# Six pieces of the second down projection as block products of seven factors, with all sums of quarters on GpSimd

## Chip, cores, metric

One core of a Trainium2 chip runs the whole program. The metric is the device time of one launch in microseconds.

## What is computed

Two transformer blocks, one behind the other, on 256 tokens of width 1024. The change is in the last product of the second one:

```python
def second_block(x, ...):
    ...
        h = h + y @ w_out[l]
        u = _rms(h, ln_ffn_g[l])
        h = h + jnp.square(jax.nn.relu(u @ w_ff1[l])) @ w_ff2[l]
    return h
```

`w_ff1` is 1024 x 4096 and `w_ff2` 4096 x 1024. With `relu(..)**2` called the hidden values (256 tokens x 4096), the last step is a product 256 x 4096 x 1024, added to `h`. All inputs are fp32.

## The kernel before

TensorE multiplies in fp32r. To keep the precision, each operand of the large products is split in two parts, high (the value rounded by a ScalarE copy) and low (the rest, by a VectorE subtraction), and `product3` (from L701; its matmul is L707) issues three matmuls for each product: high x high, high x low, low x high.

**The second down projection** is the stage "down2". Its contraction length 4096 is 32 tiles of 128. Two tiles are a *piece*; there are 16 pieces, called 0 to 15 here (`c` in the code). A piece of weights is 128 partitions x 2048: two k-tiles of 1024 output columns. The weights arrive by SyncE's DMA in chunks of two pieces (2 MB) into three ring slots; a slot is loaded again once both its pieces are split (`pieces_split`).

**ScalarE** (`split_high`, to L1743) writes the high part of a piece into one of two buffers (W_HIGH) when TensorE has read the piece two before (`down2_pieces_read`). **VectorE** (`split_low`, L2318 to L2325) then writes the low part (W_LOW), `weights - W_HIGH`, both operands in SBUF. **TensorE** (`down`, L1082 to L1105) goes over pieces 0 to 13 in order. For each, two k-tiles, four PSUM banks (two token tiles x two halves of 512 output columns), three matmuls of 128x512: 24 matmuls a piece. The last two pieces (14 and 15) are done bank by bank, so that a bank's result can be scaled, added to X and stored while the next is computed.

**Before it** the stage "ffn2" computes the hidden values: `u @ w_ff1` in 32 jobs. Two jobs make two hidden tiles, called q = 0 to 15 here; q belongs to piece q of down2. ScalarE copies half a job's bank, VectorE adds (`add_cross`, L2647) and squares into one of two buffers HF2 (L3179), ScalarE and VectorE split into HID2_HIGH and HID2_LOW (L2254, L2675). In between they split the weights of the next piece, as in down2. GpSimd does nothing in either stage.

Each engine's order is that in which the code is written; semaphores link the engines.

Of the kernel before, what the change touches and what calls it, by code (L numbers as in the profile page):

```python
# [16 lines left out]
F32 = mybir.dt.float32  # L17
# [6 lines left out]
P = 128  # L24
S = 256
# [193 lines left out]
def build(nc, x, weights, params, params2, consts, tables, rel_bias, norm_final, positions, table_dram, out):  # L219
    with ExitStack() as ctx:  # L220
# [240 lines left out]
        def piece_source(k):  # L461

            kind, i, j = PIECES[k]
            width = CHUNKS[CHUNK_AT[kind, i]][2]
            rows = {"branch": 4, "down1": width // D, "down2": width // D}.get(kind, KD)
            w = rings[weight_slots(kind, i)[0]][:, 0:width].rearrange("p (k n) -> p k n", k=rows)
            if kind in ("down1", "down2"):
                return w[:, 2 * j:2 * j + 2, :]
            if (kind, i) in TOKEN_CHUNKS:
                return w[:, 4 * j:4 * j + 4, :]  # L470
            if PIECES[k] in FIRST_HIDDEN:
                return w[:, :, :].rearrange("p k (t j n) -> p k j t n", t=2, j=2)[:, :, j, :, :]
# [137 lines left out]
        def _(pe):  # L610
# [468 lines left out]
                branch_product(i)  # L1079


            def down(kind, high, low, nk, ready, fills):  # L1082
# [12 lines left out]

                for c in range(nk // 2 - 2):
                    for k in range(2):
                        ready(2 * c + k)
                        for b in range(4):
                            ins = part(c, k, b)  # L1100
                    ins.then_inc(sem(kind + "_pieces_read"), 1)
                ready(nk - 1)
                for b in range(4):
                    for c in (nk // 2 - 2, nk // 2 - 1):
                        for k in range(2):  # L1105
                            ins = part(c, k, b)
                    close_fill(ins)
# [552 lines left out]
        def _(act):  # L1660
# [60 lines left out]
            def split_high(k):  # L1721

                if k >= len(PIECES):
                    return
                kind, i, _ = PIECES[k]
                slot, turn = weight_slots(kind, i)
                if PIECES[k] == ("in1", 1, 0):
                    act.wait_ge(sem("second_weights_in"), 16)
                else:
                    act.wait_ge(sem(f"weights_in{slot}"), 16 * turn)  # L1730
                if PIECES[k] == ("in2", 0, 0):
                    act.wait_ge(sem("hidden_split"), FF1_CHUNKS)
# [10 lines left out]
                act.activation(like_source(piece_parts(k)[0], k), piece_source(k), ACT.Copy).then_inc(sem("pieces_high"), 1)  # L1743

            def norm_gains(n, banks=range(4)):

# [519 lines left out]
            hidden2_high(q)  # L2266
            for k in range(PIECE_AT["down2", 0, 0] + 2, len(PIECES)):
                split_high(k)


        @block.vector
        def _(dve):
# [45 lines left out]
            def split_low(k):  # L2318

                if k >= len(PIECES):  # L2320
                    return
                dve.wait_ge(sem("pieces_high"), k + 1)
                high, low = [like_source(part, k) for part in piece_parts(k)]
                dve.tensor_tensor(low, piece_source(k), high.bitcast(F32), ALU.subtract)\  # L2324
                    .then_inc(sem("pieces_split"), 1)  # L2325

            def norm_gains(n, banks=range(4)):

# [875 lines left out]
        def _(pool):  # L3204
# [230 lines left out]
```

## Time and profile before

| | |
|---|---|
| time, median of 3 runs | 931.65 us (931.39 to 932.35) |
| the profiled execution | 931.5 us, its span in the trace 929.6 us |
| granted TensorE clock, mean | 0.999 |
| TensorE busy | 915.3 us (98%) |
| VectorE busy | 626.2 us (67%) |
| ScalarE busy | 486.8 us (52%) |
| GpSimd busy | 65.3 us (7%) |

The span is what the instructions cover; 1.9 us lie around it. A matmul's busy time (0.39 us for 512 columns) overlaps the next one's: the distance of starts tells what one costs. Times in a timeline are microseconds from the span's start.

### The profile page before, as it was taken

The page shows a single profiled execution, that of the slowest core. Times are in us where ns is not written, and L with a number is a line of the kernel's source. Part 1 is how long each engine was busy: PE and PEld are TensorE (multiplying, and loading weights), DVE is VectorE, ACT ScalarE, POOL GpSimd, SP SyncE. Part 2 cuts the span into 40 slices and gives each one's busy share as a digit, 9 for nine tenths or more (in the row PEclk, how much of TensorE's full clock was granted, in tenths as well). Part 3 has the DMA queues.
Part 4 walks back from the last instruction along what each step waited for, and adds up shares of the span by engine and source line. Part 5 has one row for each costly group of instructions (what it writes and reads, how often), then busy time and mean ns, then how long its engine had stood idle before and what let it go on. Part 6 is the DMA issues. An engine that isn't in the chain of part 4 may idle for free.

```text
span 929.6 us, 15708 instructions
## 1 busy us (share of the span) xinstructions
PE 915.3 (98%) x6417; PEld 785.4 (84%) x6417; DVE 626.2 (67%) x1025; ACT 486.8 (52%) x767; POOL 65.3 (7%) x79
## 2 busy tenths in 40 slices
PE   9999999999999999999999999999999999999998
PEld 8999987787778788888888889988987788888886
DVE  5776446566787768777744769579767677775343
ACT  5654345547854465555534665546427455553331
POOL 1000000131004100000000000003450000000000
PEclk9999999999999999999999999999999999999999
DMA  9769852244456435544443432231002345555421
GB/s 326 298 132 278 315 182 91 99 173 146 172 215 235 181 135 204 203 183 183 181 181 129 191 141 91 91 138 47 3 3 74 126 176 195 197 200 210 183 91 45
DMA packets 16870, 149.78 MB, mean 161 GB/s; under 512 B 1744, under 2 KB 6224, under 8 KB 8352
## 3 DMA queue, kind: packets, MB, share of 16 engines
q1 hardware_dynamic: 14688, 140.24, 40.7%
q0 software_dynamic: 1296, 5.24, 3.1%
q10 hardware_dynamic: 816, 3.31, 0.9%
q8 instruction: 51, 0.84, 0.4%
q14 instruction: 19, 0.16, 0.1%
HBM read 144.59 MB, written 4.19 MB: 160 GB/s over the span
## 4 chain that ended last, share of the span: by engine, by line
PE 89%; DVE 4%; ACT 3%; issue 2%; POOL 1%; DVEq 0%; ACTq 0%; POOLq 0%
PE bank L707 46%; PE bank L749 15%; PE bank L751 7%; PE bank L664 4%; PE bank L1509 3%; PE bank L914 1%; POOL HN L3251 1%; PE bank L951 1%; PE bank L988 1%; PE bank L811 1%; DVE W_LOW L2324 1%; PE bank L825 1%; ACT W_HIGH L1743 1%; PE bank L1376 1%; PE bank L1270 0%
## 5 line engine op out<-in xcount | busy, mean ns | idle before, releaser
L2324 DVE TENSOR_TENSOR W_LOW<-weights,W_HIGH 128x2048 fp32r<-128x2048 f32 (+1 forms) x98 | 224.5, 2292 | 141.5 <-ACT W_HIGH L1743 140.8
L1743 ACT ACTIVATE W_HIGH<-weights 128x2048 fp32r<-128x2048 f32 (+1 forms) x98 | 186.4, 1903 | 154.7 <-PE bank L707 153.2
L749 PE MATMUL bank<-OVER_BOTH,W_HIGH 128*128 128x512 f32 x608 | 211.6, 393 | 0.2 <-DVE W_LOW L2324 0.2
L751 PE MATMUL bank<-OVER_BOTH,W_LOW 128*128 128x256 f32 x608 | 170.2, 280 | 0.0
L749 PEld LDWEIGHTS bank<-OVER_BOTH,W_HIGH 128*128 128x128 f32 x608 | 114.2, 188 | 25.8 <-DVE W_LOW L2324 0.5
L751 PEld LDWEIGHTS bank<-OVER_BOTH,W_LOW 128*128 128x128 f32 x608 | 114.2, 188 | 0.0
L707 PE MATMUL bank<-W_HIGH,HID_HIGH 128*128 128x512 f32 x200 | 77.9, 390 | 0.0
L707 PE MATMUL bank<-W_LOW,HID_HIGH 128*128 128x512 f32 x200 | 77.9, 390 | 0.0
L707 PE MATMUL bank<-W_HIGH,HID_LOW 128*128 128x512 f32 x200 | 77.9, 390 | 0.0
L1681 ACT ACTIVATE ARENA<-bank 128x256 f32<-128x256 f32 x76 | 29.0, 383 | 87.2 <-PE bank L751 86.4
L707 PE MATMUL bank<-FIRST_HIGH,W_HIGH 128*128 128x256 f32 x216 | 61.6, 285 | 0.0
L707 PE MATMUL bank<-FIRST_HIGH,W_LOW 128*128 128x256 f32 x216 | 61.2, 283 | 0.0
L707 PE MATMUL bank<-FIRST_LOW,W_HIGH 128*128 128x256 f32 x216 | 61.2, 283 | 0.0
L664 PE MATMUL bank<-HT,weights 128*128 128x256 f32 x240 | 55.4, 383 | 0.0
L707 PE MATMUL bank<-GATE_HIGH,FIRST_HIGH 128*128 128x512 f32 x128 | 52.2, 408 | 1.0 <-DVE RING_LOW L2471 1.0
L707 PE MATMUL bank<-GATE_HIGH,FIRST_LOW 128*128 128x512 f32 x128 | 50.2, 392 | 0.0
L707 PE MATMUL bank<-RING_LOW,FIRST_HIGH 128*128 128x512 f32 x128 | 50.1, 391 | 0.0
L664 PEld LDWEIGHTS bank<-HT,weights 128*128 128x128 f32 x240 | 44.6, 190 | 6.5 <-issue 0.7
L2647 DVE TENSOR_TENSOR ARENA<-bank,ARENA 128x256 f32<-128x256 f32 x76 | 31.9, 421 | 25.1 <-ACT ARENA L1681 25.1
L2471 DVE TENSOR_TENSOR RING_LOW<-weights,GATE_HIGH 128x1024 fp32r<-128x1024 f32 x32 | 39.5, 1234 | 11.2 <-ACT GATE_HIGH L1778 11.2
L707 PEld LDWEIGHTS bank<-W_HIGH,HID_LOW 128*128 128x128 f32 x200 | 37.6, 188 | 7.9
L707 PEld LDWEIGHTS bank<-W_HIGH,HID_HIGH 128*128 128x128 f32 x200 | 37.6, 188 | 7.8
(524 smaller groups left out, 1827.9 us busy)
## 6 DMA issues: line engine op xcount, KB each, us to landing
weights<-weights_dram SPq DMA_DIRECT2D x62, 2048.0 KB, 7.8
weights<-weights_dram SPq DMA_DIRECT2D x3, 1024.0 KB, 9.3
bias_rows_dram<-ARENA POOLq DMA_DIRECT2D x1, 3072.0 KB, 39.3
BIAS<-params_dram ACTq DMA_DIRECT2D x1, 1997.0 KB, 13.6
weights<-weights_dram SPq DMA_DIRECT2D x1, 1664.0 KB, 6.8
weights<-weights_dram SPq DMA_DIRECT2D x1, 1584.0 KB, 7.9
weights<-weights_dram SPq DMA_DIRECT2D x3, 512.0 KB, 5.7
X<-x_dram ACTq DMA_DIRECT2D x2, 512.0 KB, 4.1
```

The source lines that it names most:

```text
L664: ins = pe.matmul(o, w[:, k, a:a + n], HT[:, k, :], start=(k == 0), stop=(k == KD - 1))
L707: ins = pe.matmul(o, left[a][k], right[b][k], start=(first and k == 0 and a + b == 0), stop=(last and k == n - 1 and a == 1))
L749: pe.matmul(o[:, :].rearrange("p (q n) -> p q n", q=2), high, OVER_BOTH[:, :, k, :], start=(k == 0), stop=False, skip_group_check=True)
L751: ins = pe.matmul(o[:, 0:S], low, OVER_HT[:, k, :], start=False, stop=(k == KD - 1), skip_group_check=True)
L811: pe.matmul(BK[0][:, 0:P], zeros, zeros, start=True, stop=True)
L825: ins = pe.matmul(o[:, t * S:(t + 1) * S], w[b][:, k, t * P:(t + 1) * P], first[a][:, k, :], start=(k + a + b + t == 0), stop=(b == 1 and ...
L1509: ins = pe.matmul(o[b:b + HD, n * HD:(n + 1) * HD], left[b:b + HD, 4 * g + n, :], right[b:b + HD, 4 * g + n, :], start=True, stop=True)
L1681: act.activation(CROSS[kind][:, n % 2, :], o[:, 0:S], ACT.Copy).then_inc(sem("cross_by_act"), 1)
L1743: act.activation(like_source(piece_parts(k)[0], k), piece_source(k), ACT.Copy).then_inc(sem("pieces_high"), 1)
L2324: dve.tensor_tensor(low, piece_source(k), high.bitcast(F32), ALU.subtract)\
L2471: dve.tensor_tensor(low, src, high.bitcast(F32), ALU.subtract).then_inc(sem("gate_split"), 1)
L2647: job_out(dve.tensor_tensor(dst[:, half], o[:, S:2 * S], CROSS[kind][:, n % 2, :], ALU.add), (kind, *tile))
```

## The change

A piece is a product of 2 x 2 blocks: the hidden values in quarters a[t][k] (token tile t, k-tile k, 128x128) and the weights in quarters b[k][f] (k-tile k, column half f, 128x512). Before it takes 8 block products. For the pieces 2, 4, 6, 8, 10 and 12 (`SEVEN`) it now takes 7 (Winograd's form), some of them of sums of quarters:

- **GpSimd** computes four sums of hidden quarters (128x128 each) for each of the six, in ffn2, once q's hidden values are ready; and, in down2, four sums of weight quarters (128x512 each), straight from the ring. The third sum reads the first two's results and the fourth the third's, by way of semaphores. It writes them raw into W_RAW; there are two places for weight sums, in HT/HN (place 0) and in the ARENA (place 1). `W_SUMS_AT` gives the six pieces the places 0, 0, 1, 0, 1, 0.
- **ScalarE** splits the hidden sums (one 128x512 copy) and the weight sums (two of 128x1024) as it does all operands, and **VectorE** subtracts as often. A place is written again when the piece that used it was read (`wait_sums_place`). The fourth weight quarter is needed in no product by itself, so the piece's own split shrinks from 2048 to 1536 columns.
- **TensorE** issues 21 matmuls in place of 24 for each of the six: three of the products go straight to down2's banks 4 and 5 and (the last) 6, others are summed over the six pieces in banks 0 to 3. The first three products need no weight sum.
- **At the end** ScalarE copies bank 0 and VectorE adds banks 0 to 3 into X by eight instructions (two sums, six multiply-adds), ahead of the ones that add banks 4 to 7.
- VectorE, before it writes an HF2 buffer again, waits for GpSimd's sums from it too.

```diff
+SEVEN = (2, 4, 6, 8, 10, 12)
...
+        W_SUMS_AT = [0, 0, 1, 0, 1, 0]
...
+        def wait_sums_place(eng, n):
+
+            if n == 0:
+                eng.wait_ge(sem("jobs_written"), len(JOBS))
+            elif n == W_SUMS_AT.index(1):
+                eng.wait_ge(sem("down2_pieces_read"), 4)
+            else:
+                last = max(m for m in range(n) if W_SUMS_AT[m] == W_SUMS_AT[n])
+                eng.wait_ge(sem("down2_pieces_read"), SEVEN[last] + 1)
...
+            def seven_products(c, high, low):
...
+                product(BK[0], hidden(0, 0), weights_at(0, 0), True)
+                product(BK[4], hidden(0, 1), weights_at(1, 0), False)
+                pe.wait_ge(sem("hidden_sums_split"), n + 1)
+                product(BK[5], [part[:, 3, :] for part in hid], weights_at(1, 1), False)
+                for at, o, left in ((0, BK[1], 0), (1, BK[3], 2), (2, BK[2], 1), (3, BK[6], None)):
+                    pe.wait_ge(sem("weight_sums_split"), 2 * n + at // 2 + 1)
+                    ins = product(o, hidden(1, 1) if left is None else [part[:, left, :] for part in hid],
+                                  [part[:, at, :] for part in sums], left is not None)
+                return ins
...
                 for c in range(nk // 2 - 2):
-                    for k in range(2):
-                        ready(2 * c + k)
-                        for b in range(4):
-                            ins = part(c, k, b)
+                    if kind == "down2" and c in SEVEN:
+                        ready(2 * c + 1)
+                        ins = seven_products(c, high, low)
+                    else:
+                        for k in range(2):
+                            ready(2 * c + k)
+                            for b in range(4):
+                                ins = part(c, k, b)
                     ins.then_inc(sem(kind + "_pieces_read"), 1)
...
+                n = seven(k)
+                if n is not None:
+                    high = W_SUMS[W_SUMS_AT[n]][0]
+                    wait_sums_place(act, n)
+                    for q in range(2):
+                        act.wait_ge(sem("weight_sums"), 3 * n + 2 * q + 1)
+                        act.activation(flat(high[:, 2 * q:2 * q + 2, :]), flat(W_RAW[W_SUMS_AT[n]][:, 2 * q:2 * q + 2, :]), ACT.Copy)\
+                            .then_inc(sem("weight_sums_high"), 1)
...
+                if n is not None:
+                    (high, low), sums = W_SUMS[W_SUMS_AT[n]], W_RAW[W_SUMS_AT[n]]
+                    dve.wait_ge(sem("weight_sums"), 3 * n + 3)
+                    for q in range(2):
+                        dve.wait_ge(sem("weight_sums_high"), 2 * n + q + 1)
+                        half = slice(2 * q, 2 * q + 2)
+                        dve.tensor_tensor(flat(low[:, half, :]), flat(sums[:, half, :]), flat(high[:, half, :]).bitcast(F32),
+                                          ALU.subtract).then_inc(sem("weight_sums_split"), 1)
...
+            for n, c in enumerate(SEVEN):
...
+                pool.wait_ge(sem(f"weights_in{slot}"), 16 * turn)
+                wait_sums_place(pool, n)
+                pool.tensor_tensor(sums[:, 1, :], b[1][1], b[0][1], ALU.subtract)
+                pool.tensor_tensor(sums[:, 0, :], b[0][1], b[0][0], ALU.subtract).then_inc(sem("weight_sums"), 1)
+                pool.wait_ge(sem("weight_sums"), 3 * n + 1)
+                pool.tensor_tensor(sums[:, 2, :], b[1][1], sums[:, 0, :], ALU.subtract).then_inc(sem("weight_sums"), 1)
+                pool.wait_ge(sem("weight_sums"), 3 * n + 2)
+                pool.tensor_tensor(sums[:, 3, :], b[1][0], sums[:, 2, :], ALU.subtract).then_inc(sem("weight_sums"), 1)
```

VectorE before, in down2, pieces 3 to 7 (W_LOW_71 and W_LOW_72 are the two buffers of low parts):

```order
L2324 TENSOR_TENSOR W_LOW_71<-weights,W_HIGH_65 128x2048 [waits pieces_high]
L2324 TENSOR_TENSOR W_LOW_72<-weights,W_HIGH_66 128x2048 [waits pieces_high]
L2324 TENSOR_TENSOR W_LOW_71<-weights,W_HIGH_65 128x2048 [waits pieces_high]
L2324 TENSOR_TENSOR W_LOW_72<-weights,W_HIGH_66 128x2048 [waits pieces_high]
L2324 TENSOR_TENSOR W_LOW_71<-weights,W_HIGH_65 128x2048 [waits pieces_high]
```

VectorE of the change at the same place, pieces 3 to 7 (L2411 is `split_low`'s old line, W_SUMS_LOW_120 place 0 and W_SUMS_LOW_122 place 1 of the weight sums):

```order
L2411 TENSOR_TENSOR W_LOW_71<-weights,W_HIGH_65 128x2048 [waits pieces_high]
L2411 TENSOR_TENSOR W_LOW_72<-weights,W_HIGH_66 128x1536 [waits pieces_high]
L2419 TENSOR_TENSOR W_SUMS_LOW_120<-HN,W_SUMS_HIGH_119 128x1024 [waits weight_sums_high,weight_sums]
L2419 TENSOR_TENSOR W_SUMS_LOW_120<-HN,W_SUMS_HIGH_119 128x1024 [waits weight_sums_high]
L2411 TENSOR_TENSOR W_LOW_71<-weights,W_HIGH_65 128x2048 [waits pieces_high]
L2411 TENSOR_TENSOR W_LOW_72<-weights,W_HIGH_66 128x1536 [waits pieces_high]
L2419 TENSOR_TENSOR W_SUMS_LOW_122<-ARENA,W_SUMS_HIGH_121 128x1024 [waits weight_sums_high,weight_sums]
L2419 TENSOR_TENSOR W_SUMS_LOW_122<-ARENA,W_SUMS_HIGH_121 128x1024 [waits weight_sums_high]
L2411 TENSOR_TENSOR W_LOW_71<-weights,W_HIGH_65 128x2048 [waits pieces_high]
```

Behind the low part of each even piece now stand two subtractions of sums, the first of which waits for all of that piece's weight sums, and the next odd piece's low part stands behind them.

GpSimd of the change, the weight sums of pieces 4 and 6 (before, GpSimd has no instruction here):

```order
L3455 TENSOR_TENSOR HN<-weights 128x512 [waits down2_pieces_read,weights_in1]
L3456 TENSOR_TENSOR HN<-weights 128x512
L3458 TENSOR_TENSOR HN<-weights,HN 128x512 [waits weight_sums]
L3460 TENSOR_TENSOR HN<-weights,HN 128x512 [waits weight_sums]
L3455 TENSOR_TENSOR ARENA<-weights 128x512 [waits down2_pieces_read,weights_in2]
L3456 TENSOR_TENSOR ARENA<-weights 128x512
L3458 TENSOR_TENSOR ARENA<-weights,ARENA 128x512 [waits weight_sums]
L3460 TENSOR_TENSOR ARENA<-weights,ARENA 128x512 [waits weight_sums]
```

Piece 4's set (in HN, place 0) waits until piece 2 is read, piece 6's (ARENA, place 1) until piece 3 is read; it stands right behind piece 4's.

ScalarE of the change, pieces 3 to 5 of down2 (before: three copies of 128x2048):

```order
L1811 ACTIVATE W_HIGH_65<-weights 128x2048 [waits down2_pieces_read,weights_in0]
L1811 ACTIVATE W_HIGH_66<-weights 128x1536 [waits down2_pieces_read,weights_in1]
L1819 ACTIVATE W_SUMS_HIGH_119<-HN 128x1024 [waits weight_sums,down2_pieces_read]
L1819 ACTIVATE W_SUMS_HIGH_119<-HN 128x1024 [waits weight_sums]
L1811 ACTIVATE W_HIGH_65<-weights 128x2048 [waits down2_pieces_read,weights_in1]
```

The copy of piece 5 now stands behind two copies that wait for GpSimd.

## Rows read from the trace of the kernel before

**Rows 1.** The page: span, busy time by engine, weight loads (us to landing)

```profile
span 929.6 us, 15708 instructions
...
PE 915.3 (98%) x6417; PEld 785.4 (84%) x6417; DVE 626.2 (67%) x1025; ACT 486.8 (52%) x767; POOL 65.3 (7%) x79
...
weights<-weights_dram SPq DMA_DIRECT2D x62, 2048.0 KB, 7.8
```

**Rows 2.** Chain that ended last, from 740 us: start, us, what

```profile
838.10 87.34 PE bank L707 x384
...
925.46 0.48 DVE X L3195
```

**Rows 3.** Timeline of TensorE in down2: start, us, instruction [idle before it]

```profile
837.93 0.39 PE L707 MATMUL bank<-W_HIGH,HID_HIGH 128*128 128x512 f32 x1
...
843.15 0.39 PE L707 MATMUL bank<-W_HIGH,HID_LOW 128*128 128x512 f32 x1
843.37 0.39 PE L707 MATMUL bank<-W_HIGH,HID_HIGH 128*128 128x512 f32 x1
...
915.45 0.46 PE L707 MATMUL bank<-DOWN_HIGH,HID_HIGH 128*128 128x512 f32 x1
```

**Rows 4.** Timelines of ScalarE and VectorE, end of ffn2 and down2

```profile
843.63 1.92 ACT L1743 ACTIVATE W_HIGH<-weights 128x2048 fp32r<-128x2048 f32 x1 [2.80 <-PE bank L707]
849.07 1.92 ACT L1743 ACTIVATE W_HIGH<-weights 128x2048 fp32r<-128x2048 f32 x1 [3.52 <-PE bank L707]
...
834.80 2.29 DVE L2324 TENSOR_TENSOR W_LOW<-weights,W_HIGH 128x2048 fp32r<-128x2048 f32 x1 [0.65 <-ACT W_HIGH L1743]
...
839.01 0.69 DVE L3179 SCALAR_TENSOR_TENSOR ARENA<-ARENA 128x512 f32<-128x512 f32 x1
...
845.58 2.29 DVE L2324 TENSOR_TENSOR W_LOW<-weights,W_HIGH 128x2048 fp32r<-128x2048 f32 x1 [2.33 <-ACT W_HIGH L1743]
...
913.07 2.28 DVE L2324 TENSOR_TENSOR DOWN_LOW<-weights,DOWN_HIGH 128x2048 fp32r<-128x2048 f32 x1
...
922.69 0.75 DVE L2651 SCALAR_TENSOR_TENSOR X<-bank,STAT,X 128x512 f32<-128x512 f32 x1 [2.04 <-PE bank L707]
925.46 0.88 DVE L3195 SCALAR_TENSOR_TENSOR X<-bank,STAT,X 128x256 f32<-128x256 f32 x2 [2.02 <-PE bank L707]
```

**Rows 5.** Timelines: GpSimd without VectorE beside it; ScalarE on 1024 columns

```profile
200.15 1.97 POOL L3237 TENSOR_TENSOR ARENA<-ARENA 128x384 f32<-128x384 f32 x2 [4.06 <-PE bank L959]
285.97 1.29 POOL L3251 TENSOR_TENSOR HN<-HN,ARENA 128x512 f32<-128x512 f32 x1 [58.31 <-DVE ARENA L2608]
306.39 2.56 POOL L3251 TENSOR_TENSOR HN<-HN,ARENA 128x512 f32<-128x512 f32 x2 [2.83 <-DVE ARENA L2608]
...
292.04 1.04 ACT L1943 ACTIVATE YT_HIGH<-ARENA 128x1024 fp32r<-128x1024 f32 x1
```

**Rows 6.** Timelines of GpSimd and VectorE where both work

```profile
295.47 2.22 POOL L3251 TENSOR_TENSOR HN<-HN,ARENA 128x512 f32<-128x512 f32 x1 [2.82 <-DVE ARENA L2608]
297.65 3.42 POOL L3251 TENSOR_TENSOR HN<-HN,ARENA 128x512 f32<-128x512 f32 x1
178.91 2.98 POOL L3237 TENSOR_TENSOR ARENA<-ARENA 128x384 f32<-128x384 f32 x2 [79.96 <-PE bank L988]
...
286.74 2.68 DVE L2324 TENSOR_TENSOR W_LOW<-weights,W_HIGH 128x2048 fp32r<-128x2048 f32 x1 [0.85 <-ACT W_HIGH L1743]
295.32 1.21 DVE L2590 TENSOR_TENSOR YT_LOW<-ARENA,YT_HIGH 128x1024 fp32r<-128x1024 f32 x1
297.62 2.29 DVE L2324 TENSOR_TENSOR W_LOW<-weights,W_HIGH 128x2048 fp32r<-128x2048 f32 x1 [0.49 <-ACT W_HIGH L1743]
301.17 0.69 DVE L2608 SCALAR_TENSOR_TENSOR ARENA<-ARENA,bank 128x512 f32<-128x512 f32 x1 [0.66 <-POOL HN L3251]
179.73 1.28 DVE L2471 TENSOR_TENSOR RING_LOW<-weights,GATE_HIGH 128x1024 fp32r<-128x1024 f32 x1
```

**Rows 7.** Groups of GpSimd: busy us, mean ns of one, idle before

```profile
L3251 POOL TENSOR_TENSOR HN<-HN,ARENA 128x512 f32<-128x512 f32 x9 | 14.5, 1634 | 66.8 <-DVE ARENA L2608 66.8
```

More of the change, by code:

```diff
@@ L405, in build, with raw @@
         Y_GD = HT[:, 5:8, :]
+        HID_SUMS = [(over(f"HID_SUMS_HIGH{n}", place, at, [4, P]), over(f"HID_SUMS_LOW{n}", place, at + 512, [4, P]))
+                    for n, (place, at) in enumerate([("BIAS", 1024 * i) for i in range(4)] + [("NF", 0), ("SM8", 0)])]
+        W_SUMS = [(over("W_SUMS_HIGH0", "HT", 0, [4, 512]), over("W_SUMS_LOW0", "HN", 0, [4, 512])),
+                  (over("W_SUMS_HIGH1", "ARENA", 8192, [4, 512]), over("W_SUMS_LOW1", "ARENA", 16384, [4, 512]))]
+        W_SUMS_AT = [0, 0, 1, 0, 1, 0]
+        def raw(place, at, n, w):
+            return place[:, at:at + n * w].rearrange("p (a b) -> p a b", a=n)
+        BIAS_ROWS, HN_ROWS = [t[:, :, :].rearrange("p a b -> p (a b)") for t in (BIAS, HN)]
+        HID_RAW = [raw(BIAS_ROWS, 1024 * i + 512, 4, P) for i in range(4)] + [raw(NF, 512, 4, P), raw(SM8, 512, 4, P)]
+        W_RAW = [raw(HN_ROWS, 0, 4, 512), raw(ARENA, 16384, 4, 512)]
         def y2_low(k):
@@ L474, in piece_source, with seven, part_of @@
             return w[:, :, j * n:min((j + 1) * n, width // rows)]
+        def seven(k):
+            kind, i, j = PIECES[k]
+            return SEVEN.index(2 * i + j) if kind == "down2" and 2 * i + j in SEVEN else None
+        def part_of(t, k):
+            if seven(k) is None:
+                return t
+            return t.rearrange("p k n -> p (k n)")[:, 0:1536]
+        def wait_sums_place(eng, n):
[6 more added lines that the diff above has]
+                eng.wait_ge(sem("down2_pieces_read"), SEVEN[last] + 1)
         FIRST_HIDDEN = [(kind, 0, j) for kind in ("ffn1", "ffn2") for j in range(2)]
@@ L1079, in _, with product, hidden, weights_at @@
                 branch_product(i)
+            def seven_products(c, high, low):
+                n = SEVEN.index(c)
+                w, hid, sums = split_piece("down2", c // 2, c % 2), HID_SUMS[n], W_SUMS[W_SUMS_AT[n]]
+                if n == 0:
+                    for b in range(4):
+                        pe.wait_ge(sem(f"job_out{b}"), len(range(b, len(JOBS), 4)))
+                def product(o, left, right, own):
+                    return product3(o[:, :], [[part] for part in left], [[part] for part in right],
+                                    first=own and n == 0, last=own and n == len(SEVEN) - 1)
+                def hidden(t, k):
+                    return [part[:, 2 * c + 1 - k, t * P:(t + 1) * P] for part in (high, low)]
+                def weights_at(k, f):
+                    return [part[:, 1 - k, f * 512:(f + 1) * 512] for part in w]
+                product(BK[0], hidden(0, 0), weights_at(0, 0), True)
[7 more added lines that the diff above has]
+                return ins
             def down(kind, high, low, nk, ready, fills):
@@ L1096, in down @@
                 for c in range(nk // 2 - 2):
-                    for k in range(2):
-                        ready(2 * c + k)
-                        for b in range(4):
-                            ins = part(c, k, b)
+                    if kind == "down2" and c in SEVEN:
[4 more added lines that the diff above has]
+                            ready(2 * c + k)
+                            for b in range(4):
+                                ins = part(c, k, b)
                     ins.then_inc(sem(kind + "_pieces_read"), 1)
@@ L1742, in split_high @@
                     wait_piece_used(act, k - 2)
[L1743 removed]
+                act.activation(part_of(like_source(piece_parts(k)[0], k), k), part_of(piece_source(k), k), ACT.Copy)\
+                    .then_inc(sem("pieces_high"), 1)
+                n = seven(k)
[6 more added lines that the diff above has]
+                            .then_inc(sem("weight_sums_high"), 1)
             def norm_gains(n, banks=range(4)):
@@ L2250, in _, with hidden_sums_high @@
                 half_squares(4, tt, 1)
+            def hidden_sums_high(n):
+                act.wait_ge(sem("hidden_sums"), 3 * n + 3)
+                act.activation(flat(HID_SUMS[n][0]), flat(HID_RAW[n]), ACT.Copy).then_inc(sem("hidden_sums_high"), 1)
             def hidden2_high(q):
+                if q - 1 in SEVEN:
+                    hidden_sums_high(SEVEN.index(q - 1))
                 act.wait_ge(sem("hidden_ready"), FF1_CHUNKS + q + 1)
@@ L2268, in _ @@
                 split_high(k)
+            act.wait_ge(sem("hidden_split"), FF1_CHUNKS + FF2_KT // 2)
+            act.wait_ge(sem("down2_pieces_read"), SEVEN[-1] + 1)
+            act.activation(HF2[:, 0, :], BK[0][:, :], ACT.Copy).then_inc(sem("cross_by_act"), 1)
         @block.vector
@@ L2321, in split_low @@
                     return
+                n, src = seven(k), piece_source(k)
                 dve.wait_ge(sem("pieces_high"), k + 1)
-                high, low = [like_source(part, k) for part in piece_parts(k)]
-                dve.tensor_tensor(low, piece_source(k), high.bitcast(F32), ALU.subtract)\
+                high, low = [part_of(like_source(part, k), k) for part in piece_parts(k)]
+                dve.tensor_tensor(low, part_of(src, k), high.bitcast(F32), ALU.subtract)\
                     .then_inc(sem("pieces_split"), 1)
+                if n is not None:
[6 more added lines that the diff above has]
+                                          ALU.subtract).then_inc(sem("weight_sums_split"), 1)
             def norm_gains(n, banks=range(4)):
@@ L3166, in _, with hidden_sums_low @@
             link(dve.reciprocal(RSTD, SUMSQ))
+            def hidden_sums_low(n):
+                high, low = HID_SUMS[n]
+                dve.wait_ge(sem("hidden_sums_high"), n + 1)
+                dve.tensor_tensor(flat(low), flat(HID_RAW[n]), flat(high).bitcast(F32), ALU.subtract)\
+                    .then_inc(sem("hidden_sums_split"), 1)
             def hidden2_low(q):
+                if q - 1 in SEVEN:
+                    hidden_sums_low(SEVEN.index(q - 1))
                 hidden_low(HID2_HIGH, HID2_LOW, slice(2 * q, 2 * q + 2), HF2[:, q % 2, :], FF1_CHUNKS + q)
@@ L3175, in _ @@
                     dve.wait_ge(sem("hidden_split"), FF1_CHUNKS + q - 1)
+                    if q - 2 in SEVEN:
+                        dve.wait_ge(sem("hidden_sums"), 3 * SEVEN.index(q - 2) + 3)
                 add_cross("ffn2", n, (c, j, t), m)
@@ L3188, in _, with gain @@
                 split_low(k)
+            def gain(tt, dc, src):
+                xs = X[:, tt, dc * 512:(dc + 1) * 512]
+                return dve.scalar_tensor_tensor(out=xs, in0=src, scalar=RSTD[:, tt:tt + 1], in1=xs, op0=ALU.mult, op1=ALU.add)
+            dve.wait_ge(sem("down2_pieces_read"), SEVEN[-1] + 1)
+            dve.wait_ge(sem("cross_by_act"), 4 * (FF1_CHUNKS + FF2_CHUNKS) + 1)
+            link(dve.tensor_tensor(HF2[:, 1, :], BK[2][:, :], HF2[:, 0, :], ALU.add))
+            gain(0, 0, HF2[:, 0, :])
+            link(gain(0, 1, HF2[:, 1, :]))
+            link(dve.tensor_tensor(HF2[:, 0, :], BK[3][:, :], HF2[:, 1, :], ALU.add))
+            gain(0, 1, BK[1][:, :])
+            gain(1, 0, HF2[:, 0, :])
+            link(gain(1, 1, HF2[:, 0, :]))
+            link(gain(1, 1, BK[1][:, :]))
             for b in range(3):
@@ L3315, in _ @@
                 masks("gd", lv)
+            for n, q in enumerate(SEVEN):
+                pool.wait_ge(sem("hidden_ready"), FF1_CHUNKS + q + 1)
+                low = HID_RAW[n]
+                a = [[HF2[:, q % 2, (1 - k) * S + t * P:(1 - k) * S + (t + 1) * P] for k in range(2)] for t in range(2)]
+                pool.tensor_tensor(low[:, 2, :], a[0][0], a[1][0], ALU.subtract)
+                pool.tensor_tensor(low[:, 0, :], a[1][0], a[1][1], ALU.add).then_inc(sem("hidden_sums"), 1)
+                pool.wait_ge(sem("hidden_sums"), 3 * n + 1)
+                pool.tensor_tensor(low[:, 1, :], low[:, 0, :], a[0][0], ALU.subtract).then_inc(sem("hidden_sums"), 1)
+                pool.wait_ge(sem("hidden_sums"), 3 * n + 2)
+                pool.tensor_tensor(low[:, 3, :], a[0][1], low[:, 1, :], ALU.subtract).then_inc(sem("hidden_sums"), 1)
+            for n, c in enumerate(SEVEN):
+                k = PIECE_AT["down2", c // 2, c % 2]
+                src, sums = piece_source(k), W_RAW[W_SUMS_AT[n]]
+                b = [[src[:, 1 - j, f * 512:(f + 1) * 512] for f in range(2)] for j in range(2)]
+                slot, turn = weight_slots(*PIECES[k][0:2])
+                pool.wait_ge(sem(f"weights_in{slot}"), 16 * turn)
[6 more added lines that the diff above has]
+                pool.tensor_tensor(sums[:, 3, :], b[1][0], sums[:, 2, :], ALU.subtract).then_inc(sem("weight_sums"), 1)
 def kernel(**inputs):
```

## The prediction

> **What bounds the kernel now.** I read the page first: TensorE is busy 98% of the span, the others 67, 52 and 7% [rows 1]. The chain that ended last says the same of this place: from 838.10 it is 87.34 us of L707 matmuls, 384 of them, without a break, and then one VectorE instruction [rows 2]. So in down2 a matmul that is left out is worth its full distance, as long as nobody makes TensorE wait. The timeline of TensorE gives that distance: piece 0 starts at 837.93, piece 1 at 843.37, 5.44 us for 24 matmuls, or 0.2267 us each [rows 3]. (The 0.39 us behind each start overlap the next.)
>
> Next I asked how much room the helpers have. ScalarE starts the copy for piece 2 at 843.63, 0.26 us after TensorE goes to piece 1; VectorE's part is 845.58 + 2.29 = 847.87 [rows 4]; TensorE reaches piece 2 at 837.93 + 2 x 5.44 = 848.81. TensorE wakes 0.10 us after VectorE is done (DOWN_LOW ends at 913.07 + 2.28 = 915.35, its matmul starts at 915.45 [rows 3, 4]). Room: 848.81 - 847.87 - 0.10 = 0.84 us a piece. The zero idle time on TensorE hides that this is little.
>
> **What is removed.** Six pieces lose three matmuls: 18 x 0.2267 = 4.08 us. A piece of 21 lasts 4.76 us, which also shortens the time in which the next (odd) piece must be split: its room falls from 0.84 to 0.16 us.
>
> **What is added, by length.** ScalarE: 1.04 us for 1024 columns [rows 5], 1.92 for 2048 [rows 4], so about 1.48 for 1536; per even piece 1.48 + 2 x 1.04 in place of 1.92. VectorE: 1.21 for 1024 [rows 6], 2.29 for 2048; 1.75 + 2 x 1.22 in place of 2.29. Over two pieces (10.2 us) that is VectorE 6.5, ScalarE 5.5: both fit by throughput. GpSimd: 128x512 takes 1.28 us (1.29 alone, 2.56 for two), 128x384 0.98 [rows 5], so about 2.3 ns a column and 0.4 us for 128x128. A set of weight sums is 4 x 1.28 plus two waits on itself, 5.3 us.
>
> **What it costs in waits.** The trace shows how GpSimd and VectorE get on. A GpSimd 128x512 add asked for at 295.47 took 2.22 us: VectorE's YT_LOW subtraction ran from 295.32 to 296.53, and 296.53 + 1.16 is where the add ended. The next, at 297.65, took 3.42: W_LOW ran 297.62 to 299.91, and it ended 1.16 behind that. The other way, a W_LOW at 286.74 took 2.68 in place of 2.29, since a GpSimd add held until 287.26. An instruction with only one operand in SBUF (301.17, bank and ARENA) kept its 0.69 [rows 6]. So a GpSimd sum and a VectorE subtraction of two SBUF operands run one after the other, each holding the other off for its whole length but the last 0.12 us. At 179.73 VectorE asked while the first of two GpSimd instructions ran, and got in between them (1.28 for 1.22; the pair 2.98 for 1.97) [rows 5, 6]: who asked first goes first. All of `split_low` and all new subtractions are of that kind, and so are all GpSimd sums.
>
> The Trainium skill has this rule in "SBUF — State Buffer", section on who interferes with whom: the port pair that VectorE and GpSimd share is an exclusive lock for a whole instruction, also for a VectorE instruction with two SBUF inputs against a GpSimd one that reads SBUF. By it the sum is the +3.4 below; were the two free of each other it would be -3.4. The rows bear the rule out.
>
> Now the timetable, t = 0 where TensorE starts piece 3 (the set for piece 4 may then start, since piece 2 is read):
> - ScalarE copies piece 4: 0.26 to 1.74. GpSimd sums 1 and 2: 0.28 to 2.80. VectorE wants piece 4's low part at 1.77, gets in at 2.67, ends 4.43. GpSimd sum 3: 4.32 to 5.60 (held off by VectorE), sum 4: 5.68 to 6.96. Weights of pieces 4 and 5 are there: loads land after 7.8 us [rows 1] and are issued two chunks ahead.
> - VectorE may subtract from 7.06. But GpSimd's next set (piece 6, place 1, free since t = 5.7) stands right behind and begins at 6.92; VectorE gets in at 8.07 and ends 9.30. TensorE, in piece 4 since 5.44, needs the first weight sums after nine matmuls, at 7.48, and goes on at 9.40: **wait 1.92**.
> - The second half: held off again until 10.34, done 11.57, TensorE goes on at 11.67 and not at 10.76: **0.91**.
> - Piece 5's low part, held off until 12.61, done 14.90; TensorE starts piece 5 at 15.00 and not at 13.03: **1.97**.
>
> From piece 6 on GpSimd is ahead with its sums, and only collisions are left. Piece 7: VectorE wants to split it 2.2 us into piece 6, GpSimd's third sum for piece 8 took the port 0.5 us before, 0.63 lost against a room of 0.16: wait **0.47**. Carried on in the same way, piece 9 waits **1.71** (piece 8's own sums are subtracted late) and piece 11 **0.47**. Behind piece 12 GpSimd has nothing left. Piece 1 of down2 costs **0.04**: GpSimd starts piece 2's set with the last ffn2 job, pushes the square of 839.01 and the split behind it by 0.7, against about the same room. Sum of waits 7.49, less 4.08: **+3.4 us**.
>
> This rests on GpSimd's 1.28 us. Worked through with other lengths: 1.12 gives +0.4, 1.20 +1.8, 1.24 +2.6, 1.36 +3.9, 1.40 +4.7. The mean of L3251 is 1.634 us [rows 7], but includes time held off, so it would count that twice; as an upper bound it gives +9.9. The lower bound is no collision at all (below). I take 1.28, read from three instructions of this very shape. "GPSIMD Engine Reference" of the Trainium skill, section on performance versus the Vector engine, gives 4497 ns for 2048 columns; a quarter, 1.12 us, is an estimate from that page, which by itself would make the change +0.4, and rows 5 speak against it.
>
> **Costed at nothing.** Hidden sums in ffn2: 24 GpSimd instructions of 0.4 us, six copies (0.6) and six subtractions (0.7). There W_LOW ended at 834.80 + 2.29 = 837.09 and piece 0 was needed at 837.93 [rows 3, 4]: a room of 0.84, and one short GpSimd sum in the way takes 0.1 to 0.4. Without that cover it would be at most six times 0.4. The end: eight VectorE instructions of about 0.75 [rows 4], 6 us, run behind piece 15's low part. TensorE then has four banks of 2.79 us left; VectorE is done with them some 4 us after bank 4's result, catches up with banks 4, 5 and 6, and is free some 2 us before the last bank. The last store is not later; uncovered it would be up to 2 us.
>
> **Rivals.**
> - *The port does not collide* with these sums (they read the ring), so the sums lie beside the matmuls. Only piece 4's set is still late: its four sums end at 5.5, ScalarE's second copy keeps it from piece 5 until 6.6 where it could start at 5.7, TensorE waits 0.7. -4.08 + 0.7 = -3.4, time 928.1. It decides if the waits stay below 4.08. For: TensorE is the bound and 4.08 is sure. Against: rows 6, with W_LOW itself. Chance 0.13.
> - *Pieces 4 and 5 only*: the later sets fall into VectorE's idle time. +4.8 - 4.08 = +0.7, time 932.2. For: VectorE sits idle 2.33 us before a split there [rows 4]; against: odd pieces have 0.16 us of room, and four sums hit it somewhere. Chance 0.20, with GpSimd somewhat faster than 1.28 in it.
> - *GpSimd is slower* on ring operands or loses more turns, 1.4 to 1.64: +4.7 to +9.9, time up to 941.4. Chance 0.07.
> - *The forecast*, waits at 4, 5 and at odd pieces, +1.4 to +5. Chance 0.60.
>
> **How the numbers follow.** The profiled execution took 931.5, 929.6 of it the span; the median of the runs is 931.65, no different. 931.5 + 3.4 = 934.9. The forecast's own range is 933 to 936.5. For eight in ten I go down to the first rival's 928.1, since it is the only case on the other side, and up to 939.5, halfway into the slow case. A measurement of this kernel can tell 0.2% (1.9 us) from nothing: faster than 929.8 is the first rival, 0.13; within, the second, some of the forecast's low end, 0.21; slower 0.66.
>
> **What would show it.** Right: 18 matmuls fewer in down2; TensorE idle some 2, 1 and 2 us inside piece 4 and before piece 5, released by VectorE's W_SUMS_LOW and W_LOW; 0.5 to 1.7 before 7, 9, 11; GpSimd 128x512 from 1.3 to 3.4 us each; W_LOW of 2.3 to 3.4; the end as before, 0.5 us of VectorE. Wrong: GpSimd's sums of 1.28 us beside a running W_LOW; a wait at piece 2 or in ffn2; a distance of matmuls above 0.2267 in the seven products, as their bank changes each time (it does before, too, at no cost); VectorE's additions behind the last bank.

## The result, and the profile after

The change takes 935.14 us (median of 5 runs, 934.89 to 935.46) against 931.79 before (931.39 to 932.35): slower, ratio 1.0036, 95% interval 1.0023 to 1.0049. The span is 932.8 against 929.6 [rows 1].

The page of the change, the same lines as [rows 1]:

```profile
span 932.8 us, 15782 instructions
...
PE 913.3 (98%) x6399; PEld 780.8 (84%) x6399; DVE 663.6 (71%) x1051; ACT 500.0 (54%) x786; POOL 141.2 (15%) x127
```

There are 18 matmuls less, and TensorE is still at 98%. GpSimd's busy time grew by 76 us, VectorE's by 37. Neither is work alone: 24 weight sums of 1.28 us and 24 short ones of 0.46 would be 42 us of GpSimd, and VectorE, with the same instructions but no weight sums beside it, is only 20 us above the kernel before (646.1, experiment 1).

The chain of the change from the start of down2 (start, us, what); before it was one unbroken piece of 384 matmuls [rows 2]:

```profile
837.98 21.47 PE bank L743 x93
859.45 0.03 issue
859.47 0.02 POOLq L507
859.49 1.29 POOL HN L3460
860.78 0.02 issue
860.80 4.52 DVE W_SUMS_LOW L2419 x2
865.32 3.31 DVE W_LOW L2411
868.62 0.14 issue
868.76 10.47 PE bank L743 x45
...
880.83 0.97 DVE W_LOW L2411
881.81 1.27 issue
883.08 4.54 DVE W_SUMS_LOW L2419 x2
887.62 3.32 DVE W_LOW L2411
890.94 0.14 issue
891.07 10.46 PE bank L743 x45
...
901.61 27.18 PE bank L743 x117
928.80 0.02 issue
928.82 0.48 DVE X L3315
```

It leaves TensorE twice for long: at piece 4 through GpSimd's last sum, both subtractions of sums and piece 5's low part, and before piece 9 through the same instructions of VectorE. Two subtractions of 1.22 us take 4.5 us there, a low part of 2.29 takes 3.3.

TensorE in piece 4 and at the start of piece 5 (start, us, instruction, idle before it):

```profile
861.09 0.39 PE L743 MATMUL bank<-W_HIGH,HID_SUMS_LOW 128*128 128x512 f32 x1
863.14 0.50 PE L743 MATMUL bank<-W_SUMS_HIGH,HID_SUMS_HIGH 128*128 128x512 f32 x1 [1.67 <-DVE W_SUMS_LOW L2419]
863.48 0.40 PE L743 MATMUL bank<-W_SUMS_LOW,HID_SUMS_HIGH 128*128 128x512 f32 x1
...
864.41 0.40 PE L743 MATMUL bank<-W_SUMS_HIGH,HID_SUMS_LOW 128*128 128x512 f32 x1
865.37 0.50 PE L743 MATMUL bank<-W_SUMS_HIGH,HID_SUMS_HIGH 128*128 128x512 f32 x1 [0.56 <-DVE W_SUMS_LOW L2419]
...
866.64 0.40 PE L743 MATMUL bank<-W_SUMS_HIGH,HID_LOW 128*128 128x512 f32 x1
868.76 0.47 PE L743 MATMUL bank<-W_HIGH,HID_HIGH 128*128 128x512 f32 x1 [1.72 <-DVE W_LOW L2411]
```

Read the starts and take off 0.227: 863.14 - 861.09 gives 1.83 us lost, then 0.73 and 1.89. After each long wait the first matmul costs another 0.11 or 0.08.

GpSimd and VectorE over pieces 3 to 5:

```profile
854.09 1.30 POOL L3455 TENSOR_TENSOR HN<-weights 128x512 f32<-128x512 f32 x1 [7.97 <-PE bank L743]
855.34 1.30 POOL L3456 TENSOR_TENSOR HN<-weights 128x512 f32<-128x512 f32 x1
856.72 2.69 POOL L3458 TENSOR_TENSOR HN<-weights,HN 128x512 f32<-128x512 f32 x1
859.48 1.28 POOL L3460 TENSOR_TENSOR HN<-weights,HN 128x512 f32<-128x512 f32 x1
860.72 1.28 POOL L3455 TENSOR_TENSOR ARENA<-weights 128x512 f32<-128x512 f32 x1
861.97 2.27 POOL L3456 TENSOR_TENSOR ARENA<-weights 128x512 f32<-128x512 f32 x1
864.31 2.15 POOL L3458 TENSOR_TENSOR ARENA<-weights,ARENA 128x512 f32<-128x512 f32 x1
...
855.56 2.69 DVE L2411 TENSOR_TENSOR W_LOW<-weights,W_HIGH 128x1536 fp32r<-128x1536 f32 x1 [2.12 <-ACT W_HIGH L1811]
860.80 4.52 DVE L2419 TENSOR_TENSOR W_SUMS_LOW<-HN,W_SUMS_HIGH 128x1024 fp32r<-128x1024 f32 x2 [2.55 <-POOL HN L3460]
```

They alternate. The low part asked at 855.56 and ends at 858.25 (2.69 in place of 1.76), after GpSimd's second sum. GpSimd's third asked at 856.72 and took 2.69, held off by that low part. Then piece 6's first sum starts at 860.72, 0.08 us before VectorE asks at 860.80, and goes first.

### The profile page after: what moved, and what is told of

Same layout as the page of the kernel before. It is cut to its first block, busy times and chain, and to the rows that moved or that the text cites. A ratio compares the mean times of both kernels' runs of the same rounds, so it can differ in the third digit from the quotient of the medians.

```text
span 932.8 us, 15782 instructions
## 1 busy us (share of the span) xinstructions
PE 913.3 (98%) x6399; PEld 780.8 (84%) x6399; DVE 663.6 (71%) x1051; ACT 500.0 (54%) x786; POOL 141.2 (15%) x127
## 4 chain that ended last, share of the span: by engine, by line
PE 87%; DVE 6%; ACT 3%; issue 2%; POOL 1%; DVEq 0%; ACTq 0%; POOLq 0%
PE bank L743 44%; PE bank L785 15%; PE bank L787 7%; PE bank L700 4%; PE bank L1577 3%; DVE W_LOW L2411 2%; PE bank L950 1%; POOL HN L3371 1%; DVE W_SUMS_LOW L2419 1%; PE bank L987 1%; PE bank L1024 1%; PE bank L847 1%; ACT W_HIGH L1811 1%; PE bank L861 1%; PE bank L1444 1%
## 5 line engine op out<-in xcount | busy, mean ns | idle before, releaser
L2411 DVE TENSOR_TENSOR W_LOW<-weights,W_HIGH 128x2048 fp32r<-128x2048 f32 (+1 forms) x98 | 229.6, 2344 | 114.7 <-ACT W_HIGH L1811 113.9
L1811 ACT ACTIVATE W_HIGH<-weights 128x2048 fp32r<-128x2048 f32 (+1 forms) x98 | 183.9, 1877 | 144.2 <-PE bank L743 142.8
L743 PE MATMUL bank<-W_HIGH,HID_HIGH 128*128 128x512 f32 x164 | 64.3, 392 | 3.1 <-DVE W_LOW L2411 3.0
L743 PE MATMUL bank<-W_HIGH,HID_LOW 128*128 128x512 f32 x164 | 63.9, 390 | 0.0
L743 PE MATMUL bank<-W_LOW,HID_HIGH 128*128 128x512 f32 x164 | 63.9, 389 | 0.0
L1893 ACT ACTIVATE ARENA<-bank 128x256 f32<-128x256 f32 (+4 forms) x50 | 20.6, 429 | 41.9 <-PE bank L1577 23.5
L743 PEld LDWEIGHTS bank<-FIRST_HIGH,W_HIGH 128*128 128x128 f32 x216 | 41.4, 192 | 0.8 <-issue 0.6
```

Source lines behind the costliest of these rows:

```text
L743: ins = pe.matmul(o, left[a][k], right[b][k], start=(first and k == 0 and a + b == 0), stop=(last and k == n - 1 and a == 1))
L1811: act.activation(part_of(like_source(piece_parts(k)[0], k), k), part_of(piece_source(k), k), ACT.Copy)\
L1893: fill_out(act.activation(dst, o[0:rows, 0:n], ACT.Copy, scale=scale), name)
L2411: dve.tensor_tensor(low, part_of(src, k), high.bitcast(F32), ALU.subtract)\
```

## The experiments

All times are medians of interleaved runs against the kernel before (931.74 to 931.88). The stretch of down2, from its first matmul's start to its last's, is worked out from the timelines of TensorE as in [rows 3]: 87.09 us before (837.93 to 925.03), 90.57 in the change (837.82 to 928.39).

**1. The same work without GpSimd's weight sums.** ScalarE and VectorE split plain quarters; the six pieces' results are left wrong.

```diff
-                        act.wait_ge(sem("weight_sums"), 3 * n + 2 * q + 1)
-                        act.activation(flat(high[:, 2 * q:2 * q + 2, :]), flat(W_RAW[W_SUMS_AT[n]][:, 2 * q:2 * q + 2, :]), ACT.Copy)\
+                        act.activation(flat(high[:, 2 * q:2 * q + 2, :]), piece_source(k)[:, q, :], ACT.Copy)\
...
-                    dve.wait_ge(sem("weight_sums"), 3 * n + 3)
...
-            for n, c in enumerate(SEVEN):
...
```

> GpSimd computes no weight sums; ScalarE and VectorE split plain quarters of the piece in their place, with the same number and size of instructions, and TensorE keeps its 21 matmuls (so the six pieces' results are left wrong). If the loss comes from GpSimd's sums (the port and their lateness), all waits inside pieces 4 to 11 go: 18 matmuls of 0.2267 us are saved less some tenths for restarts, 927.8 to 928.3. If the added work of ScalarE and VectorE is what costs, it stays at 932 to 935.

928.69 us, ratio 0.9964 (0.9952 to 0.9976). down2 took 83.68 us, 3.41 less than before. The starts of its matmuls show one wait, 0.18 us before piece 11. So ScalarE's and VectorE's added work costs next to nothing by itself; the whole loss hangs on GpSimd's sums, by the port or by their lateness. The time is 0.4 us above the expectation.

**2. The sums alone, in the kernel before.** GpSimd computes all 24, nobody uses them; waits keep the ring and place 0 safe.

```diff
+                    if was == "down2" and 2 * n in SEVEN:
+                        sp.wait_ge(sem("weight_sums"), 3 * SEVEN.index(2 * n) + 3)
...
+            for n, c in enumerate(SEVEN):
...
+                pool.tensor_tensor(sums[:, 1, :], b[1][1], b[0][1], ALU.subtract)
...
```

> The kernel before, plus GpSimd's 24 weight sums, which nobody uses: the port's collisions without anything else. By the timetable the old room of 0.84 us a piece hides nearly all of them: +0.3, 932.1. If collisions cost time by themselves, whatever the room: +2 to +3, 934 to 935.

931.51 us, ratio 0.9997 (0.9988 to 1.0006): the time does not show them. The collisions are there; groups of VectorE in its down2 (busy us, mean ns):

```profile
L2345 DVE TENSOR_TENSOR W_LOW<-weights,W_HIGH 128x2048 fp32r<-128x2048 f32 x14 | 36.5, 2610 | 35.5 <-ACT W_HIGH L1764 35.5
```

The mean low part takes 2.61 us in place of 2.29. The room of 0.84 us a piece takes nearly all of that up, but not the longest, for piece 5:

```profile
862.54 3.27 DVE L2345 TENSOR_TENSOR W_LOW<-weights,W_HIGH 128x2048 fp32r<-128x2048 f32 x1 [2.65 <-ACT W_HIGH L1764]
...
865.54 0.39 PE L728 MATMUL bank<-W_HIGH,HID_LOW 128*128 128x512 f32 x1
865.96 0.47 PE L728 MATMUL bank<-W_HIGH,HID_HIGH 128*128 128x512 f32 x1
```

The two starts are 0.42 us apart, 0.19 more than the usual 0.227, though the row shows no idle time. Before piece 1 it is 0.15. down2 took 87.74 us in this trace, 0.65 more than before, where +0.3 was expected. The time hides that: the span ends 3.67 us after the last matmul's start (926.03), and 4.59 before (925.03); in every other run here it is 4.4 to 4.6, and why it is shorter in this one is open. So the port alone costs some tenths; for the loss of the change it needs a VectorE with more to do and pieces with less room.

**3. Five pieces, from piece 4.** No set of sums is late for its piece now.

```diff
-SEVEN = (2, 4, 6, 8, 10, 12)
+SEVEN = (4, 6, 8, 10, 12)
...
-        W_SUMS_AT = [0, 0, 1, 0, 1, 0]
+        W_SUMS_AT = [0, 1, 0, 1, 0]
```

> Five pieces (4, 6, 8, 10, 12) with the places 0, 1, 0, 1, 0, so that no set of sums is late for its piece. By the timetable the waits before odd pieces stay (0.3, 1.8, 0.5, 1.7 before 5, 7, 9, 11), less 15 matmuls or 3.4: +0.9, 932.7. If the late set of piece 4 was the whole loss, only the gain is left: 928.5 to 929.5.

933.05 us, ratio 1.0012 (1.0003 to 1.0021). The starts of its matmuls show 0.33, 1.61, 0.14 and 1.48 us lost before 5, 7, 9, 11 (expected 0.3, 1.8, 0.5, 1.7). The late set was a part of the loss; the odd pieces alone, 3.56 us, eat the whole gain of 15 x 0.2267 = 3.40.

**4. Each set held back until the one before is subtracted.**

```diff
                 wait_sums_place(pool, n)
+                if n:
+                    pool.wait_ge(sem("weight_sums_split"), 2 * n)
```

> The change, with each set of weight sums held back until VectorE has subtracted the set before. By the timetable piece 4's first wait falls from 1.9 to 0.9 and its second to nothing, the wait before 5 stays 1.9, and 7, 9, 11 wait 1.1 each: +2.6, 934.4. If the sets in each other's way were the whole cause, 4.8 us of waits would go: 930 to 931. If the order of the sets did not matter: 935.1.

934.61 us, ratio 1.0027 (1.0017 to 1.0037). Lost: 0.77 in piece 4, 1.93 before 5, then 0.96, 0.89 and 0.99 before 7, 9 and 11. Order helps a little; the time GpSimd holds the port is the same and only hits elsewhere.

**5. Memsets in place of the sums.** Nearly as late, but without reading SBUF (the six pieces' results are left wrong).

```diff
-                pool.tensor_tensor(sums[:, 1, :], b[1][1], b[0][1], ALU.subtract)
-                pool.tensor_tensor(sums[:, 0, :], b[0][1], b[0][0], ALU.subtract).then_inc(sem("weight_sums"), 1)
+                def stand_in(slot):
+                    pool.memset(sums[:, slot, :], 0.0).then_inc(sem("stand_ins"), 1)
+                    stood[0] += 1
+                    pool.wait_ge(sem("stand_ins"), stood[0])
+                    return pool.memset(sums[:, slot, :], 0.0)
+
+                stand_in(1)
+                stand_in(0).then_inc(sem("weight_sums"), 1)
...
```

> GpSimd fills each weight sum's place with two chained memsets (an estimate of 0.5 us each by the 0.26 us of 192 columns) in place of a subtraction: about as late as the sums, but reading nothing from SBUF (the six pieces' results are left wrong). If the port collisions are what counts and a memset does not collide, only lateness is left: -3.4 plus a few tenths, 928.4 to 929.2. If lateness is what counts, or a memset holds the port too: 933 to 936.

928.35 us, ratio 0.9965 (0.9951 to 0.9979); down2 83.42. GpSimd and VectorE for piece 4 in this run:

```profile
854.10 0.53 POOL L3457 MEMSET HN<- 128x512 f32 x1 [11.21 <-PE bank L743]
...
856.32 0.53 POOL L3457 MEMSET HN<- 128x512 f32 x1
...
858.07 0.53 POOL L3460 MEMSET HN<- 128x512 f32 x1
859.54 0.53 POOL L3457 MEMSET ARENA<- 128x512 f32 x1 [0.94 <-PE bank L743]
860.13 0.53 POOL L3460 MEMSET ARENA<- 128x512 f32 x1
...
855.60 1.76 DVE L2411 TENSOR_TENSOR W_LOW<-weights,W_HIGH 128x1536 fp32r<-128x1536 f32 x1 [2.12 <-ACT W_HIGH L1811]
858.63 2.36 DVE L2419 TENSOR_TENSOR W_SUMS_LOW<-HN,W_SUMS_HIGH 128x1024 fp32r<-128x1024 f32 x2 [1.27 <-POOL HN L3460]
```

The set ends 4.5 us after its start and VectorE waits for it, and then nothing holds anyone off: 1.76 and 2.36 are the free lengths, with memsets running beside all of the low part and beside the second of the two subtractions, and the memsets keep their 0.53. It is not quite as late as the sums (they would end at 5.3 unhindered), so 0.8 us of lateness is not covered by this run. VectorE ends piece 5's low part here at 863.82, and TensorE, which wants it at 864.10, has some 0.1 us to spare; 0.8 us more of lateness could thus have cost up to 0.7 us by itself, as in the first rival of the prediction. No run separates that part of the loss from the port's.

**6. One more sum a set.**

```diff
+                pool.tensor_tensor(sums[:, 1, :], b[1][1], b[0][1], ALU.subtract).then_inc(sem("done_twice"), 1)
+                pool.wait_ge(sem("done_twice"), n + 1)
                 pool.tensor_tensor(sums[:, 1, :], b[1][1], b[0][1], ALU.subtract)
```

> The change, with the first sum of each set computed twice: 5 x 1.28 us a set. By the timetable the collisions grow to 1.7 before each of 7, 9, 11, 0.8 before 3 and 2.8 in piece 4: +7.6, 939.4. If only GpSimd's lateness at piece 4 counted: 1.3 more than the change, 936.4. If the sums are mostly hidden: 935.5.

939.38 us, ratio 1.0081 (1.0067 to 1.0095). That is 4.2 us more than the change for six sums of 1.28 us, 0.7 us each on the mean, but not evenly. By the starts of its matmuls 0.45 us are lost before piece 3, 2.83 and 0.71 in piece 4, 0.85 before 5, and 1.61, 1.40 and 1.50 before 7, 9 and 11 (expected 0.8, 2.8 and three times 1.7). Before 9 the added sum costs nothing (1.42 in the change), nor does piece 12's.

Behind the wait of 2.83 us, the longest in down2 of any run here, the granted clock fell to half, which is 1.2 GHz (stretch; us, busy us of PE, PEld, DVE, ACT, POOL; clock, DMA, GB/s):

```profile
867.40:870.80 3.40, 3.09 (x8) 1.93 (x7) 3.40 (x2) 0.00 (x0) 3.32 (x2) 0.52 0.00 0
```

Its matmuls are 0.427 us apart there. It cost hardly anything, since piece 5 had to wait for its low part until 871.75 anyway.

**7. The weight sums by VectorE,** each set ahead of the same piece's low part.

```diff
+                if n is not None:
...
+                    wait_sums_place(dve, n)
+                    dve.tensor_tensor(sums[:, 1, :], b[1][1], b[0][1], ALU.subtract)
+                    dve.tensor_tensor(sums[:, 0, :], b[0][1], b[0][0], ALU.subtract).then_inc(sem("weight_sums"), 1)
...
                 dve.wait_ge(sem("pieces_high"), k + 1)
```

> The change with the 24 weight sums by VectorE, each set ahead of the same piece's low part (0.7 us a sum in place of GpSimd's 1.28 and its turns at the port); GpSimd keeps the hidden sums. VectorE then has 9.3 us of work in the 10.2 us of two pieces. By the timetable nothing waits: -4.1, and 0.5 to 1 back for what the run without weight sums also lacked: 928.2 to 928.8. If a full VectorE makes TensorE wait before each odd piece by half a microsecond or more: 930.5 to 932.

928.10 us, ratio 0.9965 (0.9953 to 0.9978): faster than both kernels, by 3.7 and 7.0 us. TensorE in its down2 has no wait at all (busy us of PE, PEld, DVE, ACT, POOL; clock, DMA, GB/s), and VectorE's sums take 0.69 us:

```profile
839.00:907.00 68.00, 68.00 (x301) 55.95 (x300) 57.52 (x53) 34.96 (x28) 0.00 (x0) 1.00 0.44 160
...
L2423 DVE TENSOR_TENSOR W_LOW<-weights,W_HIGH 128x2048 fp32r<-128x2048 f32 x9 | 20.6, 2293 | 11.2 <-ACT W_HIGH L1811 11.2
...
L2416 DVE TENSOR_TENSOR HN<-weights 128x512 f32<-128x512 f32 x4 | 2.7, 684 | 0.0
```

VectorE is busy 85% of this stretch, and that is still cheaper than sharing: the change's low parts of 2048 columns take 2742 ns and its subtractions in the ARENA 2307 in place of 1220 (its groups in down2):

```profile
L2411 DVE TENSOR_TENSOR W_LOW<-weights,W_HIGH 128x2048 fp32r<-128x2048 f32 x8 | 21.9, 2742 | 7.5 <-ACT W_HIGH L1811 7.5
...
L2419 DVE TENSOR_TENSOR W_SUMS_LOW<-ARENA,W_SUMS_HIGH 128x1024 fp32r<-128x1024 f32 x4 | 9.1, 2307 | 0.0
```

**8. Four pieces, all sums on GpSimd.**

```diff
-SEVEN = (2, 4, 6, 8, 10, 12)
+SEVEN = (4, 6, 10, 12)
...
-        W_SUMS_AT = [0, 0, 1, 0, 1, 0]
+        W_SUMS_AT = [0, 1, 0, 1]
```

> Four pieces (4, 6, 10, 12) with the places 0, 1, 0, 1, all sums on GpSimd. 12 matmuls are 2.7 us; by the timetable 0.5 us of waits are left, so -2.2, and some tenths back: 929.8 to 930.2. If the thin room of the odd pieces behind 6 and 12 is hit as before, 931 to 932.

929.65 us, ratio 0.9979 (0.9970 to 0.9988). Only piece 5 waits, 0.33 us. GpSimd can do the sums if the sets are far enough apart; two sets less turn +3.35 us into -2.14.

**9 and 10. X, HN and HT moved by 32 bytes and all behind them by 64,** in the kernel before and in the one with VectorE's sums.

```diff
+        sb("pad0", [P, 8])
         X = sb("X", [P, TT, D])
...
+        sb("pad1", [P, 8])
         STAT = sb("STAT", [P, 64])
```

> The kernel before with X, HN and HT 32 bytes further on in SBUF and all else 64. In all traces a matmul of 128x512 whose moving operand lies in HT or HN takes 0.231 to 0.234 us, and 0.2267 with one from the ARENA. If it is the address against 64 bytes, DOWN's matmuls fall to 0.2267 and those of ffn1 and ffn2 with OVER_BOTH from 0.347 to 0.340 a pair: 608 pairs, -4 us, 927.7. If it has another cause: no change, 931.8.

> Sums by VectorE and the move by 32 bytes together: the sum of the two, so 924 to 925 if the address counts, and the time of the run with VectorE's sums, 928.2 to 928.8, if not.

934.36 us (1.0032, 1.0019 to 1.0045) and 930.58 (0.9990, 0.9981 to 0.9999). Neither of the two outcomes expected came: both are some 2.5 us slower than their twins, and the matmuls with DOWN's parts stay at 0.232 us, 0.2335 before (the last 47 distances of down2 are 10.89 us, 10.93 before). See the last section.

## Why the prediction was right

Predicted 934.9, measured 935.14. By its steps, with distances of matmul starts in the change's trace:

- *Gain.* 18 matmuls less; pieces of 21 without a wait last 4.76 to 4.84 us. Right, but those with sums in place 0 give 0.08 less (below).
- *Lengths.* GpSimd 1.28 to 1.30 free, ScalarE 1.49 and 1.04 to 1.06, VectorE 1.76: right. 128x128 took 0.46.
- *The port.* Right: on one side 1.76 and 2.36 us beside memsets, on the other 2.69 and 4.52 beside sums; who asked first went first. That the reads from SBUF are what the two share fits the memsets, which write the same places and read nothing; another difference between the two instructions was not tested. The Trainium skill's rule ("SBUF — State Buffer", who interferes with whom) limits the lock of a VectorE instruction with two SBUF inputs to a GpSimd one that reads SBUF, and the memset run agrees.
- *Waits at pieces 4 and 5.* 1.92, 0.91 and 1.97 predicted, 1.83, 0.73 and 1.89 measured, and 0.30 more for the three restarts. The prediction took 0.10 us from VectorE's end to TensorE's start, read at 915.45; but TensorE was due there anyway (914.09 + 6 x 0.2267 = 915.45), so that row shows no waking. Where it does wait, the chain has 0.14, which makes the rooms 0.80 and 0.12.
- *Odd pieces.* 0.47, 1.71, 0.47 before 7, 9, 11 predicted; 0.23, 1.42, 0.25 measured, so this term was 0.75 too large. Piece 1: 0.04 predicted, 0.16 measured. VectorE before piece 9, on the sums of piece 8 and the low part, just as drawn:

```profile
883.08 4.54 DVE L2419 TENSOR_TENSOR W_SUMS_LOW<-HN,W_SUMS_HIGH 128x1024 fp32r<-128x1024 f32 x2
887.55 3.38 DVE L2411 TENSOR_TENSOR W_LOW<-weights,W_HIGH 128x2048 fp32r<-128x2048 f32 x1
```

- *Sum.* Pieces 0 to 13 take 79.64 us against 76.16 (14 x 5.44): +3.5, predicted +3.4. The waits are 6.5 and not 7.5; 1.0 us that I had not in the sum, restarts (0.6) and slower matmuls with operands in place 0 (0.3) for the most part, made up for it. That the sum is better than its terms is luck.
- *Costed at nothing.* ffn2 from its first matmul to down2's first took 89.98 us in both. Held-off sums (2.39 us for one of 0.46) stayed in VectorE's idle time. At the end VectorE was free in time, as before [rows 4]:

```profile
926.05 0.75 DVE L2746 SCALAR_TENSOR_TENSOR X<-bank,STAT,X 128x512 f32<-128x512 f32 x1 [0.21 <-PE bank L743]
928.82 0.88 DVE L3315 SCALAR_TENSOR_TENSOR X<-bank,STAT,X 128x256 f32<-128x256 f32 x2 [2.03 <-PE bank L743]
```

- *Rivals.* No collision: its time, 928.1, is what the runs without reading sums gave (928.35, 928.69), but in part by chance: it had a wait of 0.7 us that these runs lack, and lacked the slower matmuls. Pieces 4 and 5 only: refuted by experiment 3, in which odd pieces alone cost 3.6 us; in the change itself 7, 9 and 11 cost 1.9, and the waits at 4 and 5 4.45. GpSimd slower: its free length was 1.28 to 1.30. The estimate of 1.12 us from the Trainium skill's "GPSIMD Engine Reference" (section on performance versus the Vector engine) was low here by the same rows.

Experiments 3, 4, 6, 7 and 8 came out within 0.4 us of what was expected by the timetable, 1 and 2 within 0.4 and 0.6. The timetable therefore carries the explanation: neither the port nor the lateness nor the thin room alone, but GpSimd's 1.16 us holds of the port against a room of 0.16 us before odd pieces, and one late set.

## What to carry to other kernels

- Before work goes to an idle engine, ask what it shares with the busy one, and put the length of one hold against the room that the busy engine's consumer leaves. Busy shares (7% and 67%) said there was space; the room per piece, 0.84 us and then 0.16, said there was not.
- Shortening the bound engine's work also shortens every deadline behind it: 3 matmuls less are 0.68 us less room for the next split.
- Two elementwise engines on one port can be slower than the faster one alone: four sums cost VectorE 2.8 us, and GpSimd 5.1 us of the port against VectorE. Where a set must stay on GpSimd, space the sets out.

## What was not expected of the hardware

- A 128x512 matmul of the seven products takes 0.2333 us on the mean where its moving operand lies in HT or HN (place 0), and 0.2266 from the ARENA (place 1); in piece 15 of the kernel before, whose DOWN parts lie in HT and HN, it is 0.2335. It is 0.08 us a piece of place 0. Moving HT and HN by 32 bytes did not mend it and cost 2.5 us in ffn1 and ffn2. There the moving operand OVER_BOTH lies in HN and HT, and a matmul of 512 columns with W_HIGH and one of 256 with W_LOW went from 0.2301 + 0.1184 us to 0.2314 + 0.1213 on the mean of 608 pairs, which is 2.55 us. So the place in SBUF counts, by a rule that these runs do not give; open.
- A wait of TensorE costs more than its length: after it the next matmul is 0.08 to 0.11 us later in down2 of all these traces, but for the one wait at the halved clock of experiment 6.
- GpSimd's memset runs beside VectorE's subtractions of two SBUF operands without any loss to either: 0.53 us beside 1.76 and 2.36.
